# Two square projections of a two-block transformer kernel as seven quarter products (Strassen) each, with operands split in turn

## What is computed

```python
p_a = einsum('bsw,wd->bsd', out_a, w_branch_sb)      # 1024 x 1024 x 1024
p_b = einsum('bsw,wd->bsd', out_b, w_branch_ret)
merged = sigmoid(m_sb + b0) * p_a + sigmoid(m_ret + b1) * p_b
x = x + einsum('bsd,de->bse', merged, w_out)         # 1024 x 1024 x 1024
```

## Time and profile before

| | us |
|---|---|
| median of 3 runs | 2201.62 |
| lowest, highest run | 2200.14, 2207.37 |
| the profiled execution | 2203.64 |
| its span | 2201.8 |
| TensorE busy in the span | 2137.4 |
| VectorE, ScalarE, GpSimd busy | 1110.8, 938.8, 349.5 |
| granted TensorE clock, mean | 0.983 |

### The profile page before, as it was taken

The page is one execution under the profiler, slowest core; times in us unless marked ns, Lnnn a source line. Parts: engine busy times, 40 slices in busy tenths (PEclk is TensorE's granted clock), DMA queues, the critical chain, the costliest instruction groups (busy, mean ns, idle before and its releaser), DMA issues.

```text
span 2201.8 us, 29272 instructions
## 1 busy us (share of the span) xinstructions
PE 2137.4 (97%) x11719; PEld 1773.8 (81%) x11719; DVE 1110.8 (50%) x2061; ACT 938.8 (43%) x1708; POOL 349.5 (16%) x526
## 2 busy tenths in 40 slices
PE   7999989998988999999999999999999999999999
PEld 5789878876987888878888787888888878888887
DVE  5776465642465445665466645546415252434441
ACT  4665454544462425654465544642232323232220
POOL 5010361452021100000000000005103030110011
PEclk9999999998798999999999999999999999999999
DMA  4455444346613321111112211120311112343222
GB/s 141 132 177 191 128 145 133 93 108 243 233 39 110 112 72 36 37 53 58 48 39 67 63 48 39 39 71 16 116 48 53 43 50 80 113 156 133 92 92 86
DMA packets 159240, 205.57 MB, mean 93 GB/s; under 512 B 35104, under 2 KB 113408, under 8 KB 157568
## 3 DMA queue, kind: packets, MB, share of 16 engines
q1 hardware_dynamic: 139888, 136.51, 19.8%
q0 software_dynamic: 19216, 67.19, 9.3%
HBM read 148.31 MB, written 51.68 MB: 91 GB/s over the span
## 4 chain that ended last, share of the span: by engine, by line
PE 91%; DVE 4%; ACT 2%; issue 1%; DMA 1%; POOL 1%; SPq 0%; DVEq 0%; POOLq 0%; ACTq 0%
PE PS L1866 13%; PE PS L1868 13%; PE PS L1867 13%; PE PS L1859 10%; PE PS L1861 10%; PE PS L1860 10%; PE PS L1824 5%; PE PS L2148 3%; PE PS L2127 3%; PE PS L1957 1%; PE PS L2180 1%; PE PS L2193 1%; DVE WH L2583 1%; PE PS L1932 1%; PE PS L2167 1%
## 5 line engine op out<-in xcount | busy, mean ns | idle before, releaser
L1866 PE MATMUL PS<-WH,HH 128*128 128x512 f32 (+1 forms) x1344 | 532.2, 396 | 2.4 <-DVE HL L2606 1.7
L1868 PE MATMUL PS<-WH,HL 128*128 128x512 f32 (+1 forms) x1344 | 512.6, 381 | 0.0
L1867 PE MATMUL PS<-WH,HH 128*128 128x512 f32 (+1 forms) x1344 | 511.5, 381 | 0.0
L1859 PE MATMUL PS<-HH,WH 128*128 128x512 f32 (+1 forms) x1040 | 426.1, 410 | 17.7 <-DVE WH L2583 12.1
L1861 PE MATMUL PS<-HH,WH 128*128 128x512 f32 (+1 forms) x1040 | 408.3, 393 | 0.0
L1860 PE MATMUL PS<-HL,WH 128*128 128x512 f32 (+1 forms) x1040 | 407.8, 392 | 0.0
L1866 PEld LDWEIGHTS PS<-WH,HH 128*128 128x128 f32 x1344 | 253.8, 189 | 55.6 <-issue 13.2
L1868 PEld LDWEIGHTS PS<-WH,HL 128*128 128x128 f32 x1344 | 253.3, 188 | 44.6
L1867 PEld LDWEIGHTS PS<-WH,HH 128*128 128x128 f32 x1344 | 254.2, 189 | 36.9
L2583 DVE SCALAR_TENSOR_TENSOR WH<-RAW,WK,WH 128x512 fp32r<-128x512 f32 (+2 forms) x248 | 184.2, 772 | 197.1 <-ACT WH L2202 196.5
L1859 PEld LDWEIGHTS PS<-HH,WH 128*128 128x128 f32 (+1 forms) x1040 | 195.5, 188 | 60.0 <-DVE WH L2583 13.3
(11 more groups left out here) (321 smaller groups left out, 2781.6 us busy)
## 6 DMA issues: line engine op xcount, KB each, us to landing
RAW<-in_w_in SPq DMA_DIRECT2D x200, 256.0 KB, 3.2
RAW<-in_w_out SPq DMA_DIRECT2D x32, 256.0 KB, 3.5
sig_d<-WK POOLq DMA_DIRECT2D x32, 256.0 KB, 2.3
WK<-sig_d POOLq DMA_DIRECT2D x32, 256.0 KB, 3.3
WK<-in_rpb POOLq DMA_DIRECT2D x16, 480.0 KB, 4.5
RAW<-in_w_in SPq DMA_DIRECT2D x32, 192.0 KB, 4.8
dnc_d<-TM SPq DMA_DIRECT2D x12, 512.0 KB, 4.3
TM<-dnc_d SPq DMA_DIRECT2D x10, 512.0 KB, 4.2
```

The source lines that it names most:

```text
L1859: e.matmul(ps, wh, hh, start=k == 0, stop=False)
L1866: e.matmul(ps, hh, wt[:, 0:width], start=k == 0, stop=False)
L1867: e.matmul(ps, hh, wt[:, 512:512 + width], start=False, stop=False)
L1868: mm = e.matmul(ps, hl, wt[:, 0:width], start=False, stop=k == 7)
```

## The change

The blocks sb0 and sb1 become one block `sb`, and o0 and o1 one block `o`. Each is now a 2 x 2 product of quarters of 512 x 512, by the Winograd form of Strassen's scheme: seven products instead of eight, for four sums of the left quarters, four differences of the right ones and some sums of results. With left quarters A and right quarters B, in the order of the program:

| product | left (item "ya" splits it) | right (item "w") | what becomes of it |
|---|---|---|---|
| 1 | A11 | B11 | kept in U3 (ScalarE, "yx") |
| 2 | A12 | B21 | plus product 1: quarter 0 |
| 3 | S2 = S1 - A11 | T2 = B22 - T1 | plus U3: U2 ("yu") |
| 4 | S3 = A22 - S2 | T3 = T2 - B11 | plus U2: U3 |
| 5 | S1 = A21 + A22 | T1 = B12 - B11 | plus U3: quarter 1; U2 plus it: U2 |
| 6 | S4 = A12 - S2 | B22 | plus U2: quarter 2 |
| 7 | A22 | T4 = B21 - T2 | plus U3: quarter 3 |

A product is four tiles ("yp"), each of four steps of three matmuls. The left sums S1 and S2 are VectorE's, S4 and S3 (in this order) POOL's (items "ys", 128 x 2048 each); the right differences ("yt", sixteen of 128 x 512 for each projection) are POOL's. "ys" and "ya" overwrite in place, so an operand is split only when its turn comes: "ya" on ScalarE and VectorE (128 x 2048), then four "w". The branch's turned input is kept in fp32, in the place of `HH` (`HRAW`); its "st" items have no VectorE part any more. The right halves B12 and B22 come in one or two large loads ("yo", 2 MB for each projection) on SP. In `sb` the gate is multiplied on POOL ("yg", sixteen of 128 x 512). In `o` the known part U is added to the x tile on POOL ("yr", sixteen of 128 x 512), and VectorE adds the product ("ed"). The "mc" items of the second token half go away.

```diff
 RT = ["q0", "v0", "q1", "m10", "v1", "q2", "v2", "q3", "v3", "m11"]
-FIN = ["sb0", "sb1", "rt0", "rt1", "o0", "o1"]
+FIN = ["sb", "rt0", "rt1", "o"]
 BLOCKS = X + ["wo0", "wo1"] + SB + RT + FIN
...
+FIRST = [8 * b + 20 * (b > S_BLOCK) for b in range(len(BLOCKS))]
+N_W = FIRST[O_BLOCK] + 28
+QUARTERS = ((0, 0), (1, 1), (0, 1), (1, 0))
+RESULT = {1: 0, 4: 4, 5: 8, 6: 12}
+
...
+    def square(p):
+        b = SQUARE[p]
+        while prepped[0] < FIRST[b] + 8:
+            prep()
+
+        def product(j, t):
+            take(("yp", p, j, t))
+            put("yp", p, j, t)
+
+        def result(j, t):
+            put("ed", b, RESULT[j] + t)
+            if p == 0:
+                put("yg", RESULT[j] + t)
+
+        for n in range(16):
+            slot(("ed", b, n), "fin", 4)
+        for n in range(4):
+            put("fd", b, n)
+        if p == 0:
+            put("ya", 0, 1)
+        else:
+            put("ys", 1, 1)
+            put("ys", 1, 2)
+        for t in range(4):
+            product(0, t)
+            put("yx", p, t)
+            if p == 0:
+                turn_in("oa", 4 + t)
+            else:
+                put("yr", t)
+        if p == 0:
+            put("ys", 0, 1)
+            put("ys", 0, 2)
+        put("ya", p, 2)
+        right(p, 2)
+        put("ys", p, 4)
+        for c in range(4):
+            put("yt", p, 2, c)
+        put("ys", p, 3)
+        for t in range(4):
+            product(1, t)
+            result(1, t)
+            put("fd", b, 4 + t)
+        put("ya", p, 3)
+        right(p, 3)
+        for c in range(4):
+            put("yt", p, 3, c)
+        for t in range(4):
+            product(2, t)
+            put("yu", p, 2, t)
+        put("ya", p, 4)
+        right(p, 4)
+        for t in range(4):
+            product(3, t)
+            put("yu", p, 3, t)
+            if p:
+                put("yr", 4 + t)
+        put("ya", p, 5)
+        right(p, 5)
+        for t in range(4):
+            product(4, t)
+            result(4, t)
+            put("yu", p, 4, t)
+            put("fd", b, 8 + t)
+            if p:
+                put("yr", 8 + t)
...
+        for t in range(4):
+            product(5, t)
+            result(5, t)
+            put("fd", b, 12 + t)
+            if p:
+                put("yr", 12 + t)
+        for t in range(4):
+            if p == 0:
+                for n in range(3 if t == 0 else 1):
+                    prep()
+            product(6, t)
...
+
+    square(0)
+    plan.spawn(second_half())
+    gemm(BLOCK["rt0"], feeds(BLOCK["rt0"]))
+    put("yo", 1)
+    plan.spawn(merge_in())
+    gemm(BLOCK["rt1"], feeds(BLOCK["rt1"]), sums_ahead)
+    plan.drain()
+    square(1)
...
+                elif kind == "yp":
+                    p, j, t = a
+                    m, before = place[item]
+                    released(w, before)
+                    w.wait_ge(*(at["mc", 0, 4 * j + 3, "lo"] if p and j < 2 else at["ya", p, j, "lo"]))
+                    ah, al = left(p, j)
+                    for c in range(4):
+                        n = FIRST[SQUARE[p]] + 4 * j + c
...
+                        if p:
+                            hh, hl = (x[:, c, t * 128:(t + 1) * 128] for x in (ah, al))
+                            e.matmul(bank(m), hh, wt[:, 0:512], start=c == 0, stop=False)
+                            e.matmul(bank(m), hh, wt[:, 512:1024], start=False, stop=False)
+                            mm = e.matmul(bank(m), hl, wt[:, 0:512], start=False, stop=c == 3)
...
+                elif kind == "ys" and a[1] in (1, 2):
...
+                    else:
+                        w.wait_ge(*at["ys", p, 1, "s"])
+                        w.wait_ge(*(at["mc", 0, 3, "lo"] if p else at["ya", 0, 0, "lo"]))
+                        tt(a11, a21, a11, ALU.subtract).then_inc(*w.sig(*item, "s"))
+                elif kind == "ya":
+                    p, j = a
+                    w.wait_ge(*at[(*item, "hi")])
+                    hi, lo = left(p, j)
+                    tt(lo, left_raw(p, *LEFT_AT[j]), hi.bitcast(F32), ALU.subtract).then_inc(*w.sig(*item, "lo"))
...
+                        if p:
+                            w.wait_ge(*at["yr", t, "r"])
+                            w.wait_ge(c_ot[c], 16 * (t // 4))
+                            tt(ot[c], ps, sgt[fed(b, t)[0]], ALU.add).then_inc(*w.sig(*item, "out"))
+                        else:
+                            w.wait_ge(c_ob, 128)
+                            w.wait_ge(*(at["yx", 0, c, "x"] if j == 1 else at["yu", 0, 4 if j == 5 else 3, c, "u"]))
+                            u = (U2 if j == 5 else U3)[:, c * 512:(c + 1) * 512]
+                            tt(merged(cb * 4 + c, th), ps, u, ALU.add).then_inc(*w.sig(*item, "out"))
+                        continue
                     ps = bank(place["tile", b, t][0])
-                    name = BLOCKS[b]
...
+                elif kind == "ys" and a[1] > 2:
+                    p, i = a
+                    a11, a12, a22 = left_raw(p, 0, 0), left_raw(p, 1, 0), left_raw(p, 1, 1)
+                    w.wait_ge(*at["ys", p, 2, "s"])
+                    if i == 4:
+                        w.wait_ge(*(at["mc", 0, 7, "lo"] if p else at["ya", 0, 1, "lo"]))
+                        e.tensor_tensor(a12, a12, a11, ALU.subtract).then_inc(*w.sig(*item, "s"))
+                    else:
+                        w.wait_ge(*at["ys", p, 4, "s"])
+                        w.wait_ge(*at["ya", p, 2, "lo"])
+                        e.tensor_tensor(a11, a22, a11, ALU.subtract).then_inc(*w.sig(*item, "s"))
+                elif kind == "yt":
+                    p, i, c = a
+                    first = FIRST[SQUARE[p]]
+                    b11, b21, t2 = (right_raw(p, j, c) for j in range(3))
+                    b12, b22 = right_raw(p, 4, c), right_raw(p, 5, c)
+                    if i == 0:
+                        w.wait_ge(c_o1[p], 16 if p else 32)
+                        w.wait_ge(c_raw[c], raw_due[first + c])
+                        e.tensor_tensor(b12, b12, b11, ALU.subtract).then_inc(*w.sig(*item, "t"))
+                    elif i == 1:
+                        w.wait_ge(*at["yt", p, 0, c, "t"])
+                        if p:
+                            w.wait_ge(*at["w", FIRST[S_BLOCK] + 8 + c, "lo"])
+                        e.tensor_tensor(t2, b22, b12, ALU.subtract).then_inc(*w.sig(*item, "t"))
+                    elif i == 2:
+                        w.wait_ge(*at["w", first + c, "lo"])
+                        w.wait_ge(*at["yt", p, 1, c, "t"])
+                        e.tensor_tensor(b11, t2, b11, ALU.subtract).then_inc(*w.sig(*item, "t"))
+                    else:
+                        w.wait_ge(*at["w", first + 4 + c, "lo"])
+                        w.wait_ge(*at["yt", p, 1, c, "t"])
+                        e.tensor_tensor(b21, b21, t2, ALU.subtract).then_inc(*w.sig(*item, "t"))
...
+                elif kind == "yr":
+                    n = a[0]
...
+                    w.wait_ge(c_st[i], 16 * (nth + 1))
+                    if n < 4:
+                        w.wait_ge(*at["yx", 1, n, "x"])
+                    else:
+                        w.wait_ge(*at["yu", 1, 4 if 8 <= n < 12 else 3, n % 4, "u"])
+                    u = (U2 if 8 <= n < 12 else U3)[:, n % 4 * 512:(n % 4 + 1) * 512]
+                    e.tensor_tensor(sgt[i], sgt[i], u, ALU.add).then_inc(*w.sig(*item, "r"))
+                elif kind == "yg":
+                    n = a[0]
+                    th, cb, c = quarter(n)
+                    m = merged(cb * 4 + c, th)
+                    w.wait_ge(*at["ed", S_BLOCK, n, "out"])
+                    w.wait_ge(*at["ed", S_BLOCK, n, "sg"])
+                    e.tensor_tensor(m, m, sgt[fed(S_BLOCK, n)[0]], ALU.mult).then_inc(*w.sig(*item, "m"))
 
                 elif kind == "nv":
```

More of the change, by code:

```diff
@@ L149, with place_of, raw_of, operand_of @@
 X_LAST = len(X) - 1
+S_BLOCK, O_BLOCK = BLOCK["sb"], BLOCK["o"]
+SQUARE = (S_BLOCK, O_BLOCK)
+FIRST = [8 * b + 20 * (b > S_BLOCK) for b in range(len(BLOCKS))]
+N_W = FIRST[O_BLOCK] + 28
+QUARTERS = ((0, 0), (1, 1), (0, 1), (1, 0))
+RESULT = {1: 0, 4: 4, 5: 8, 6: 12}
+def place_of(n):
+    b = max(b for b in range(len(BLOCKS)) if FIRST[b] <= n)
+    return b, n - FIRST[b]
+def raw_of(n):
+    return place_of(n)[1] % NRAW
+def operand_of(n):
+    b, k = place_of(n)
+    return (SQUARE.index(b), *divmod(k, 4)) if b in SQUARE and k >= 8 else None
+def quarter(n):
+    th, cb = QUARTERS[n // 4]
+    return th, cb, n % 4
 def slot_of(n):
@@ L207 @@
 }
+GROUPS["out"] = ("yp", "yx", "yu", "yr", "yg", "ys", "yt", "ya")
 GROUP = {kind: g for g, kinds in GROUPS.items() for kind in kinds}
@@ L303, in signals @@
         "rm": [("dve", "o")],
+        "yp": [("pe", "done")],
+        "yx": [("act", "x")],
+        "yu": [("dve", "u")],
+        "yr": [("pool", "r")],
+        "yg": [("pool", "m")],
+        "ys": [("dve" if a and a[-1] in (1, 2) else "pool", "s")],
+        "yt": [("pool", "t")],
```

(4 more changed lines are left out.)

327 lines of the change are left out of this document (247 added, 80 removed).

## The result

The changed kernel takes 2230.09 us (median of 4 runs, 2224.86 to 2237.3) against 2201.96 for the kernel before (4 runs): ratio 1.0122, 95% interval [1.0101, 1.0143]. Run again beside 19 runs of the kernel before, which then had a median of 2203.89 and went from 2198.73 to 2212.21, it took 2228.72: ratio 1.0102 [1.0073, 1.013]. So the change costs 25 to 28 us. The prediction was 13.3, and its range ended at 2223: the direction was right, the size was not.

A forecast was written before the change was run, and what follows sets the result against it. TensorE, busy 97% of the span, was taken as the bound: -21.8 for matmuls, +16.4 for stalls and +18.7 for the end gave +13.3, so 2201.62 became 2214.9 us, range 2202 to 2223.

The forecast's parts named there:

- Matmuls, -21.8: Both projections together: 96 fewer matmuls on TensorE at 0.2267 us each, saving 21.8 us.
- The end, +18.7: End of the last projection: eight GpSimd rounds of store, load and addition, each waiting for its load, add 18.7 us.
- The round of 5.3: One GpSimd round at the end: store issue 0.55, load 3.3, hops 0.2, addition 1.25, together 5.3 us.
- The 0.2 for GpSimd's wake: Hops within each GpSimd round at the end, estimated at 0.2 us.
- VectorE against GpSimd: Splits finding GpSimd at work wait for its end; 512-column pairs take 1.6 us instead of 0.69; PSUM evictions pay nothing.
- rival 1: VectorE and GpSimd don't hinder each other here: stalls 5.5 us, total +0.6, time 2202; chance 0.12.
- Stalls, +16.4: TensorE waiting for late operands in the branch, at the block after it and in the last projection: 16.4 us.
- one VectorE operation ends per GpSimd operation: Read from six GpSimd additions at the kernel's start: VectorE finishes one operation soon after each GpSimd operation.
- the 2.1 and 0.9 of the prediction: Product 4 of the branch: TensorE waits 2.1 us before it and 0.9 in its first tile, 3.0 together.
- rival 3: Gaps of 2 to 3 us could bring TensorE to 1.2 GHz: up to +3.5 us, 2218; chance 0.20.
- Rival 2: End of the last projection: x1 loads land before GpSimd's additions, so no chain; -5.4 us, 2196; chance 0.08.
- TensorE over 25 us idle: Sign that the prediction is wrong: TensorE has over 25 us of idle in the changed stretch.

The follow-up runs named there:

- experiment 2: The changed kernel with the additions to x on GpSimd in the last projection placed two tiles later: 2211.57 us, ratio 1.0038 to the kernel before.
- Experiment 3: The changed kernel with GpSimd's left sums and its third and fourth kinds of right differences cut to 8 columns (output wrong): 2204.31 us, ratio 0.9995.

## Why the prediction was wrong in size

- **Matmuls, -21.8: right.** 96 rows fewer, 0.2267 each where the clock is full.
- **The end, +18.7: right.** 18.1 in the trace, 17.2 when taken away (experiment 2). The round of 5.3 measured 5.14: the load landed 3.03 to 3.86 after its issue (I had 3.3), which gave 2.56 to 3.40 of waiting, and the addition took 1.26 to 1.39. The 0.2 for GpSimd's wake came from no row; here the addition began 0.07 to 0.08 after the landing. TensorE was not held by it.
- **VectorE against GpSimd: right in kind.** Splits of 1.5 (I had 1.6), the half 4.87, evictions not hindered: rival 1 is out. (The rule of the Trainium skill, "GPSIMD Engine Reference", section "Key points", that the two engines contend at two SBUF inputs: the trace agrees, with 1.5 us instead of 0.69.) Experiment 3 shows that GpSimd's work was the cause of the long stalls; at product 3 GpSimd's part of the operands (T2) had been ready for over 20 us, so there it is the hindrance alone.
- **Stalls, +16.4: this step failed.** What each place cost, as the excess of the spacing of matmuls over 0.2267, so with the clock in it:

| place | predicted | measured |
|---|---|---|
| product 1 of the branch | 0.6 | 1.1 |
| product 3 | 5.7 | 5.7 |
| product 4 | 3.0 | 10.2 |
| start of the second branch | 1.7 | 1.7 |
| wait for the load of `ob_d` | 0 | 0.6 |
| last projection, product 3 | 2.2 | 2.2 |
| last projection, product 4 | 3.2 | 6.9 |
| sum | 16.4 | 28.4 |

With the matmuls that makes -21.8 + 28.4 = +6.6 for TensorE, where the trace has +7.3. Five of seven places are right within 0.6; nearly all of the 12.0 us that are missing, 10.9, lie at product 4, twice. (Measured in the first profile. In the second, product 3 has 6.5 and the two product 4 have about 9.0 and 6.1, so the match at product 3 is in part luck; the sum is about 1 us less.) Two steps of the working failed at product 4. First, "one VectorE operation ends per GpSimd operation": against the four differences in a row none did, and a split took 5.20 and 4.85 where I had 1.6. In the branch the first two gaps, 2.11 and 0.98, are the 2.1 and 0.9 of the prediction; the third, 3.47, is the one that this split made. I had that reading from six additions in the earlier trace rows, where it held, and took it for a rule. Second, the clock. I had it as rival 3, "up to +3.5", with 0.20, on the ground of two gaps, 3.12 and 2.56. But my own stalls were gaps of 2 to 3 us and longer, in a row. The clock fell at three places, in both profiles, behind the gap of 2.98, at those of 2.11, 0.98 and 3.47 (in the first profile before the longest of the three: the matmul of 1979.81 is slow already), and at that of 4.47. At product 3 that cost nothing in the first profile, for the splits set the pace there, and 0.9 at most in the second; at each product 4 ten or twelve matmuls lost 0.2 each, 4.4 of the 10.9 together; the late splits make the rest. It belonged in the sum.
- **Rival 2** (no chain) is out with 2.56 us of waiting and more in every round.
- **The range.** It took in the clock and slow landings, but not a larger stall, since I had walked through those instruction by instruction and held them for exact. 12 us more give 2227, which is where the runs are. What the text named as proof against it ("TensorE over 25 us idle") was near: 18.8 of gaps and 9.7 in and behind them in late matmuls.

## What to carry to other kernels

An arithmetic saving on the busiest engine is paid back wherever its operands come late; the gaps of 3.4 us and more seen here cost themselves and 1.5 to 3 us at half clock behind them, where TensorE then had its operands, and two gaps of 1.4 and 1.0 close together did once out of two times (1.7), so that belongs in the sum. When GpSimd and VectorE both take two SBUF inputs, don't price the pair by one measured pattern: a run of GpSimd instructions may hold a single VectorE instruction to its end, so place such runs where VectorE has nothing due. And read an engine's order for a load and its use next to each other: moving the use two tiles later removed 17 us at no cost.
